# Holding GpSimd's weight sums, and moving exponentials, token sums and one gate product, in a two-layer hybrid attention and mixture kernel

## What is computed

```python
z = h @ p['w_in']
(c_q, c_kv, k_pe, gq, gk, gv, dq, dk, dv, g_mla, g_gqa, g_diff) = jnp.split(z, splits, axis=-1)
o_mla = attend(q, k_mla, v_mla)
o_gqa = attend(gq, gk_all, gv_all)
o_diff = rmsnorm((a1 - lam * a2).reshape(b, t, DIFF_HEADS, DIFF_V), p['diff_subln']) * (1.0 - lam_init)
merged = (jax.nn.sigmoid(g_mla) * (o_mla @ p['w_br_mla'])
          + jax.nn.sigmoid(g_gqa) * (o_gqa @ p['w_br_gqa'])
          + jax.nn.sigmoid(g_diff) * (o_diff @ p['w_br_diff']))
y = merged @ p['w_out']
x = x + gate1 * y
x = x + gate2 * expert_choice_ffn(h2, p)
```

## Time and profile before

| what | value |
|---|---|
| runs | 1969.94, 1962.91 and 1970.39 us; median 1969.94 us |
| profiled execution | 1957.05 us, of which span 1955.0 us |
| mean granted clock of PE | 0.986 |
| busy over the span | PE 1777.1 us (91%), DVE 628.4 (32%), ACT 329.2 (17%), POOL 230.8 (12%) |
| moved | 541.08 MB, mean 277 GB/s |

### The profile page before, as it was taken

The page is one execution under the profiler, slowest core; times in us unless marked ns, Lnnn a source line. Parts: engine busy times, 40 slices in busy tenths (PEclk is TensorE's granted clock), DMA queues, the critical chain, the costliest instruction groups (busy, mean ns, idle before and its releaser), DMA issues.

```text
span 1955.0 us, 20705 instructions
## 1 busy us (share of the span) xinstructions
PE 1777.1 (91%) x8356; PEld 946.6 (48%) x8356; DVE 628.4 (32%) x1321; ACT 329.2 (17%) x811; POOL 230.8 (12%) x269
## 2 busy tenths in 40 slices
PE   6998999999999998978799989998999989898887
PEld 3556656785443332322255575576854333233222
DVE  1235235652421222221123461456424221221112
ACT  2232222320210010100032322222212101000001
POOL 0225024230000000000001430622200000000000
PEclk9999999999999999999999999999998999999999
DMA  9235132128699999999951732311457999999997
GB/s 385 77 152 217 51 144 76 65 108 345 264 377 431 428 429 428 428 428 428 425 225 44 287 115 76 119 44 70 188 220 294 407 429 428 427 428 429 429 429 296
DMA packets 59580, 541.08 MB, mean 277 GB/s; under 512 B 7192, under 2 KB 7640, under 8 KB 14560
## 3 DMA queue, kind: packets, MB, share of 16 engines
q1 hardware_dynamic: 57952, 535.65, 66.6%
q0 software_dynamic: 1536, 4.13, 0.6%
HBM read 536.54 MB, written 3.21 MB: 276 GB/s over the span
## 4 chain that ended last, share of the span: by engine, by line
PE 71%; DMA 11%; DVE 7%; ACT 4%; SPq 4%; issue 2%; DVEq 0%; ACTq 0%
PE banks L2139 23%; PE banks L1713 12%; PE banks L1751 9%; DMA ring<-in_w_exp 8%; PE banks L1777 6%; PE banks L1605 4%; PE banks L2060 3%; SPq L628 3%; DMA arena<-in_w_exp 3%; PE banks L2222 3%; ACT arena L855 2%; PE banks L1878 1%; PE banks L1660 1%; PE banks L1990 1%; PE banks L2116 1%
## 5 line engine op out<-in xcount | busy, mean ns | idle before, releaser
L2139 PE MATMUL banks<-arena 128*64 128x512 f32 x1616 | 365.1, 595 | 26.8 <-DMA arena<-in_w_exp 14.6
L2139 PE MATMUL banks<-ring,arena 128*64 128x512 f32 x1456 | 332.6, 601 | 28.6 <-DMA ring<-in_w_exp 18.8
L1713 PE MATMUL banks<-ring,arena 128*128 128x384 f32 (+1 forms) x768 | 244.1, 479 | 1.8 <-ACT arena L829 1.8
L2139 PEld LDWEIGHTS banks<-arena 128*64 128x64 f32 x1616 | 112.5, 137 | 257.5 <-issue 208.5
L2139 PEld LDWEIGHTS banks<-ring,arena 128*64 128x64 f32 x1456 | 102.1, 138 | 239.3 <-issue 189.8
L1713 PEld LDWEIGHTS banks<-ring,arena 128*128 128x128 f32 x768 | 145.8, 191 | 95.6 <-issue 2.9
L1543 DVE TENSOR_TENSOR arena<-banks,arena 32x512 f32<-32x512 f32 (+1 forms) x128 | 87.9, 687 | 274.8 <-PE banks L2139 273.4
L1777 PE MATMUL banks<-arena,ring 128*128 128x384 f32 x384 | 131.2, 499 | 7.8 <-DVE arena L1213 7.8
L1605 PE MATMUL banks<-arena 128*128 128x128 f32 (+3 forms) x740 | 106.3, 278 | 35.0 <-DVE arena L1528 18.6
L1605 PEld LDWEIGHTS banks<-arena 128*128 128x128 f32 (+3 forms) x740 | 82.6, 139 | 99.5 <-issue 39.3
L1035 ACT ACTIVATE arena<-banks 128x512 f32<-128x512 f32 x32 | 19.1, 597 | 515.8 <-PE banks L2139 515.8
(11 more groups left out here) (221 smaller groups left out, 1729.4 us busy)
## 6 DMA issues: line engine op xcount, KB each, us to landing
ring<-in_w_exp SPq DMA_DIRECT2D x75, 2048.0 KB, 28.5
arena<-in_w_exp SPq DMA_DIRECT2D x54, 2048.0 KB, 28.3
arena<-in_w_exp SPq DMA_DIRECT2D x94, 1024.0 KB, 26.7
ring<-in_w_att SPq DMA_DIRECT2D x80, 1024.0 KB, 7.6
ring<-in_w_exp SPq DMA_DIRECT2D x32, 1024.0 KB, 10.4
ring<-in_w_att SPq DMA_DIRECT2D x26, 768.0 KB, 8.6
arena<-in_w_att SPq DMA_DIRECT2D x12, 1024.0 KB, 10.9
ring<-in_w_att SPq DMA_DIRECT2D x8, 672.0 KB, 22.8
```

Of the source, the lines that this page charges most:

```text
L1713: ins = pe.matmul(ps[:, 0:width], hT[:, k, P * t:P * t + P], slots[n][:, c0:c0 + width], start=k == 0, stop=k == KC - 1)
L2139: ins = pe.matmul(PS[64 * h:64 * h + 64, bank], lhs(k), slots[i][:, c0:c0 + BF], start=k == 0, stop=k == KC - 1)
```

## The change

1. POOL: every `weight_sums` waits, beside what it waited for, until a job's probabilities are scaled: unit u of mixer 0 for job 3 + u, of mixer 1 for job 11 + u, all units of mixer 2 for job 15.
2. ACT: in each step both exponentials of the job come first, then the copy of the last job's values, then that of the next job's queries.
3. DVE: the token sums move from step 4 to step 3, ahead of the modulation rows. The reciprocals of the mean squares (line 1270, `inverse`) move in steps 14 and 15 behind the gate's last product. The transposes `("adat", 2)` and the columns that DVE makes of them move from step 5 to the end of step 7.
4. PE: in step 16 the first product of the last gate runs ahead of the values of job 15, and the last mean square comes one product later.
5. SP: the order of loads has `("gate0", 1)` ahead of the modulation and `("gate0", 2)` ahead of its second part, and the slots of the ring go round in another order.

```diff
-FILL[5].append(("adat", 2))
 for _u in range(1, 4):
     FILL[4 + _u] += [("gate", 0, _u, m) for m in PRODUCTS]
+FILL[7].append(("adat", 2))
...
-LAST_GATES = [("gate", 2, u, m) for u in range(4) for m in PRODUCTS]
-LAST_GATES.insert(2, ("square", 3))
+FILL[NJ].append(("gate", 2, 0, M5))
+LAST_GATES = [("gate", 2, u, m) for u in range(4) for m in PRODUCTS][1:]
+LAST_GATES.insert(1, ("square", 3))
...
-PLAN += [("gate0", 0)] + [("ada", 1, k) for k in range(KC)] + [("scale2", u) for u in range(4)]
-PLAN += [("gate0", u) for u in range(1, 4)]
+PLAN += [("gate0", 0), ("gate0", 1)] + [("ada", 1, k) for k in range(KC)]
+PLAN += [("gate0", 2)] + [("scale2", u) for u in range(4)] + [("gate0", 3)]
...
+                job = 3 + u if b == 0 else 11 + u if b == 1 else NJ - 1
+                pool.wait_ge(prob_ok.s, prob_ok.at(l, OUT_AT[job, 1 if JOBS[job][0] == "gqa" else 0] + 1))
                 pool.wait_ge(filled[first].s, 16 * load)
...
                 for i in range(NJ + 1):
-                    two = i < NJ and JOBS[i][0] != "mla"
-                    if two:
-                        exps(l, i, (0,))
+                    if i < NJ:
+                        exps(l, i)
+                    else:
+                        fill(l, FILL[NJ][0])
+                    if i >= 1:
+                        values(l, i - 1)
                     if i + 1 < NJ:
                         prep(l, i + 1)
-                    if i >= 1:
-                        values(l, i - 1)
-                    if i < NJ:
-                        exps(l, i, (1,) if two else (0,))
...
-                    if i >= 14:
-                        inverse(l, i - 14)
-                    if i == 4:
-                        token_sums(l)
+                    if i == NJ:
+                        inverse(l, 2)
                     for key in FILL[i]:
                         if key[0] == "gate":
                             product(l, key)
+                            if i in (14, 15) and key[3] == M4:
+                                inverse(l, i - 14)
...
                         elif key[0] in ("ada", "adat"):
+                            if key == ("ada", 1):
+                                token_sums(l)
                             modulation(l, key)
```

More of the change, by code:

```diff
@@ L178 @@
 for _i in range(NJ + 1):
+    if _i == NJ:
+        USERS += FILL[_i]
     if _i >= 1 and values_of(_i - 1):
         USERS.append(("pv", _i - 1))
-    USERS += FILL[_i]
+    if _i < NJ:
+        USERS += FILL[_i]
 USERS += LAST_GATES + [("br2", c) for c in range(KC)]
@@ L240, in placed @@
     for layer in range(DEPTH):
-        ring = sorted(range(RING), key=lambda i: (min(last.get(i & ~1, i - SLOTS), last.get(i | 1, i - SLOTS)), i))
-        ring += range(RING, SLOTS)
+        two = sorted(range(0, RING, 2), key=lambda i: min(last.get(i, i - SLOTS), last.get(i + 1, i - SLOTS)))
+        ring = [two[0], two[1], two[1] + 1, two[2], two[2] + 1, two[0] + 1] + list(range(RING, SLOTS))
         body = [u for u in PLAN if u[0] != "gain2" and (layer == 0 or u[:2] != ("ada", 0))]
-        whole = body.index(("ada", 1, KC - 1)) + 1
-        after = [ring[n % SLOTS] for n in range(whole, whole + SLOTS) if n % SLOTS < RING]
-        for n, unit in enumerate(body):
-            put(layer, [unit], [ring[n % SLOTS] if n < whole else after[(n - whole) % RING]])
+        whole = body.index(("ada", 1, KC - 1))
+        turn = [n % SLOTS for n in range(whole)] + [4, 5]
+        turn += [(0, 1, 2, 4, 3, 5)[n % RING] for n in range(len(body) - len(turn))]
+        for unit, n in zip(body, turn):
+            put(layer, [unit], [ring[n]])
         at = [place[layer, u][0] for u in body[-RING:]]
@@ L842, in user, with exps @@
                 write(PS[:, 6 + n % 2]).then_inc(user_act.s, 1)
-            def exps(l, j, maps):
+            def exps(l, j):
                 kind, _ = JOBS[j]
-                for m in maps:
+                for m in range(1 if kind == "mla" else 2):
                     n = MAP_AT[j, m]
@@ L967, in _ @@
                         nc.scalar.activation(RG, RG, ACT.Sqrt).then_inc(rootg_ok.s, 1)
-                    for key in FILL[i]:
+                    for key in FILL[i] if i < NJ else ():
                         fill(l, key)
@@ L1249, in token_sums @@
                 dve.wait_ge(ht_act.s, ht_act.at(l, 4 * NT))
-                for k in (3, 4):
+                for k in (2, 3):
                     i, _, _, use = place[l, ("ada", 1, k)]
```

## The result

Five runs of the changed kernel gave a median of 1947.58 us (1946.14 to 1951.69); five of the kernel before gave 1966.8 us (1962.91 to 1970.39). The ratio is 0.9906, 95% interval 0.9884 to 0.9928: faster by 0.9%, about 18 us. Applied to the 1969.94 us that the prediction started from, the ratio gives 1951.4 us; forecast were 1958.7, range 1948 to 1974. The 1969.94 us was a high base: 38 more runs of the kernel before, taken beside the experiments, have their middle at 1963.8 us, and only one of them is above it. The profiled execution spans 1944.3 us, 10.7 less than before.

A forecast was written before the change was run, and what follows sets the result against it. Weight transfers bound the expert part, PE the attention parts. Terms of −6.6 us in layer 0 and −4.6 in layer 1, together −11.2 us off the 1969.94 us median, gave 1958.7 us, range 1948 to 1974.

The forecast's parts named there:

- A: Step 11: holding the sums removes PE's 3.01 us wait and the slow matmuls behind it; −4.7 us in each layer.
- B: Steps 3 to 5: earlier token sums, held sums replace old waits with one; −3.6 us in layer 0, −1.6 in layer 1.
- the first rival: Most of the gain given back, including a clock drop behind step 3's new wait (+3.4 us); −2.6 us in all, chance 0.24.
- G: SP's changed order of loads: units still land in time; nothing, bound 0 to +2 us in a layer.
- D: Steps 6 to 13: value copies behind the second exponentials make PE late; +3.8 us in each layer.
- part C: Transposes ("adat", 2) and their columns move from step 5 to step 7; nothing, up to 0.2 us either way.
- E: Steps 14 and 15: later M1 against removed waits of M2 and M3 as reciprocals move; sum −1.1 us in each layer.
- F: Step 16: a product fills PE's wait for DVE's copy of job 15's values; −1.0 us in each layer.
- The cold clock behind M1's waits: Steps 12 to 15, plus step 3: new waits cool the clock; +8.0 us, 1977.9 us, chance 0.14.
- The hold does nothing: Step 11: holding the sums gains zero, the scaling stays slow or another is hit; −1.8 us, 1968.1 us, chance 0.08.
- Most is given back: Doubled copy delays in steps 6 to 9, blocked token sums, clock drop behind them; −2.6 us, 1967.3 us, chance 0.24.
- Better than my sum: Additions with two SBUF operands aren't blocked by POOL, so new waits shrink; −20.0 us, 1949.9 us, chance 0.09.

The follow-up runs named there:

- the third experiment: The changed kernel with the hold on the weight sums kept for mixer 0 alone; ratio 0.9917 to the kernel before.
- the first combination: Changed kernel with copies placed between exponentials in steps 12 to 15, token sums in step 4's gap, hold only for mixer 0 and mixer 1's first unit; ratio 0.9850.
- the second: Profile of the changed kernel run again with no edit; ratio 0.9911 to the kernel before, span 1947.7 us.

## Why the prediction was right, and where not

**A was right**, mechanism and size: −4.7 forecast, −5.0 measured, and shown by a single added wait. The slow second half of the matmuls is the clock's share, and it isn't certain: it was missing in layer 1 of the third experiment. The scaling alone takes 0.95 us, a quarter of 3.78, not a third.

**B was right in its old waits, and put the clock behind the new one at nothing.** The three old waits went. The new one came where it was put, 2.17 us for 2.8, from token sums blocked by the rotation (5.9 us for 3.8). The Trainium skill, page "SBUF — State Buffer", section "SBUF: two separate sides", says the port pair of DVE and GpSimd is locked for whole instructions by one side; the trace agrees (0.36 and 1.27 us for the two kinds of addition, 0.96 and 2.31 for the first token sum). Its figure by full exposure, 3.9 us, came out too high here. Yet layer 0 gained 2.5 us in these steps, not 3.6: the clock fell behind the new wait, which B had at nothing and only the first rival had at 1.7 us a layer, and PE waited for the ring, which G had at nothing. Both are in the rows above. Layer 1, where the clock held, came out at −1.7 for −1.6.

**D failed in one of its terms.** Taken as 0.4 us in each of steps 6 to 9 (1.6, entered as 1.5), it was nothing in 8 and 9, the steps with two maps that its reasoning was about. The 0.87 us in steps 6 and 7 have one map: 0.66 of it is ACT's order (it went with the old one), the other 0.2 stays with the held sums or with part C, and no run separates these. Steps 12 and 13 were met to 0.02 us, in step 12 by luck: M1 waited 0.86, 1.23, 1.23 and 1.95 us in the four steps where I had 1.5, 1.0, 1.0 and 1.3, and 0.46 us for M6's addition where I had 0.6. In step 12 I also took off a wait of M2, 0.67 us, that wasn't there: the three of the earlier trace rows are in steps 13 to 15. An M1 that waited 0.6 us less made up for it.

**E and F were right**, within 0.3 us: −1.0, −0.3 and −1.2 for −0.7, −0.4 and −1.0. The reciprocals alone give 3.5 us in two steps.

**G was wrong: "Nothing" for the loads.** The argument from 9.8 us of products against 8.6 us of landing holds for the ring behind the gates. It says nothing of steps 1 to 4, where the order decides which units land first. There the modulation's last units came late: 0.96 us seen, 1.3 and 0.2 us a layer when the order was undone, and up to 4.2 us (the first combination) where no other wait covered it. The bound of 0 to +2 held.

**What made the gain larger** is none of these terms. The profile of before was one of its good executions: 1957.05 us, where 37 of the 38 runs beside the experiments took longer, at a mean granted clock of 0.986, where they had 0.974 to 0.985. I subtracted its waits from a median of three runs that was itself 6 us above the middle of the 38. In steps 2 to 5 the old order loses on average 4.0 us more than that profile shows (115.4 against 111.4 in three profiles, two of them of kernels with an edit elsewhere), the new one 0.2 (107.4 against 107.2). With the 12.9 us that makes 16.7 of the 18. It goes with how often the clock fell there, eight times in three profiles against four, and with the fourth token sum, which is blocked in some places and not in others. The rest isn't located. Which part of the change steadies these steps isn't shown: no run has the hold for mixer 0 alone in the kernel before.

**The rivals.** The cold clock behind M1's waits didn't come: 1.00 in step 14 with a wait of 1.23 us. "The hold does nothing" fell with one wait. "Most is given back" had three pieces: the clock behind the wait in step 3 came, in one layer of the first profile and in both of the second; the doubled D in steps 6 to 9 and the fully blocked token sums didn't. "Better than my sum" has a time near the measured one, but by luck: it needed additions from SBUF that POOL doesn't block, and they took 1.27 us for 0.36.

## What to carry to other kernels

When two engines share a port, hold the one with slack until the other's urgent instructions are through, but only where they would meet: one hold of the four of mixer 1 had the gain, the others cost. Place each copy by whose bank is needed next, not by engine blocks; one gate copy moved ahead of the second exponentials, and the query copy behind them, were worth 5 us a layer. Before removing a wait, look for a transfer it covers: three versions here lost what they had won to weights that the changed order of loads brought late, and to the clock, which fell while PE waited for them. And before subtracting waits from a median, see whether the profile they come from is a usual one.

## What the runs showed of the hardware

- The block between DVE and POOL is mutual: the rotation's four short instructions took 1.95 us alone and 4.82 us beside DVE's token sums. A long one loses less: a weight sum, 1.27 us alone, took at most 1.46 beside the scaling of job 11, which took 3.78 for 0.95.
- It depends on where operands lie: beside a weight sum, an addition with one operand in PSUM took 0.36 us, one with both in SBUF 1.27 us (0.36 without the weight sum), and three scalings with SBUF alone 3.78 us for 0.95.
- The clock's loss behind a short wait is a matter of the execution: after nearly the same wait in step 11 it cost 1.6 us in one layer and nothing in the other, and after waits of 2.17 and 2.18 us in step 3 the clock read 0.51 in one layer and 1.00 in the other. The intervals without such waits repeated to 0.1 us.
